# Up projections of two feed-forwards: seven block products of 256 tokens for each gate/up pair

## The chip, the cores and the metric

The kernel runs on 1 core of a Trainium2 chip. The metric is the device time of one execution in microseconds: 1858.99 us, median of 3 runs (1856.67 to 1860.89). Engines are named as the profile names them: PE (TensorE, matmuls; PEld its weight loads), DVE (VectorE), ACT (ScalarE), POOL (GpSimd), SP (SyncE, which issues the loads).

## The reference

512 tokens of 1024 channels in float32 go through three residual blocks, each a mixer and a feed-forward. The feed-forward of blocks two and three, around which this case turns, is

```
def swiglu_ffn(h, w13, w2):
    g, u = jnp.split(h @ w13, 2, axis=-1)
    return (jax.nn.silu(g) * u) @ w2
x = x + swiglu_ffn(rms_norm_2(x, norm_g), w13, w2)     # w13: 1024 x 5632, w2: 2816 x 1024
```

The feed-forward of block one has a causal convolution of three taps between the up projection and silu; the mixers (four kinds of heads, a gated convolution, latent attention) are not touched.

## The kernel before

Activations lie transposed, channels on partitions: `xT` is 8 tiles of 128 channels x 512 tokens. A float32 product is made of three fp32r passes: operand = hi + lo, and `passes` (L370 to L374) adds hi*hi, hi(weight)*lo(x) and lo(weight)*hi(x) in PSUM. A weight *unit* is 1024 x 128 of a matrix: one tile of 128 output channels. For each unit SP loads `raw` (4 slots, freed by `lo_split`), ACT copies `raw` to `whi` (`split_hi`, L359), DVE makes `wlo = raw - whi` (`split_lo`, L367), both with 2 slots, and PE runs 8 x 3 matmuls of 128x128 weights and 512 columns into one of two accumulator banks (`product`, L376 on). `unit_used` tells that PE is done with a unit, `acc_free` that its bank was read out.

In `ffn2_up` and `ffn3_up` units alternate: gate tile, up tile, 22 pairs, a loop of two pairs (`pe_up`, `act_up`, `dve_up`). DVE scales each result out of PSUM by the tokens' 1/rms (`zS = ps * rs`, L622), ACT applies silu to the gate (L605), DVE multiplies (`xg`, L638), ACT copies the product to `h_hi` (L608) and POOL makes `h_lo = xg - h_hi` (L647, `pool_products`). The gain of the norm is in `xhi`, `xlo` already; 1/rms comes later through `rs`: POOL sums squares (L563), PE adds over partitions (L400, `pe_sum`, behind the first unit), ACT takes Ln and Exp (`act_rstd`, L408, L410), with a table load before (L406) and one for silu after (L588).

The order on each engine is the order in which its function issues; engines meet by semaphores alone. A wait that precedes an instruction holds all behind it on that engine.

## Time and profile before

| | |
|---|---|
| median of 3 runs | 1858.99 us |
| the profiled execution | 1858.89 us, span 1857.1 us, mean clock of PE 0.997 |
| ffn2_up, 924.6 to 1164.0 us | 239.4 us; PE busy 239.4, DVE 98.3, ACT 76.7, POOL 28.7 |
| ffn3_up, 1484.0 to 1724.0 us | 240.0 us; PE busy 239.1, DVE 99.7, ACT 76.5, POOL 29.9 |

A matmul's time in the profile is its latency; matmuls overlap, so the pace of PE is the distance of their starts. Times on POOL are rougher than on the others.

### The profile page before, as it was taken

The page shows a single profiled execution, that of the slowest core. Times are in us where ns is not written, and L with a number is a line of the kernel's source. Part 1 is how long each engine was busy: PE and PEld are TensorE (multiplying, and loading weights), DVE is VectorE, ACT ScalarE, POOL GpSimd, SP SyncE. Part 2 cuts the span into 40 slices and gives each one's busy share as a digit, 9 for nine tenths or more (in the row PEclk, how much of TensorE's full clock was granted, in tenths as well). Part 3 has the DMA queues.
Part 4 walks back from the last instruction along what each step waited for, and adds up shares of the span by engine and source line. Part 5 has one row for each costly group of instructions (what it writes and reads, how often), then busy time and mean ns, then how long its engine had stood idle before and what let it go on. Part 6 is the DMA issues. An engine that isn't in the chain of part 4 may idle for free.

```text
span 1857.1 us, 27371 instructions
## 1 busy us (share of the span) xinstructions
PE 1823.2 (98%) x10063; PEld 1475.5 (79%) x10063; DVE 916.8 (49%) x1277; ACT 716.6 (39%) x1059; POOL 210.2 (11%) x181
## 2 busy tenths in 40 slices
...
DMA packets 309228, 161.03 MB, mean 87 GB/s; under 512 B 12688, under 2 KB 306832, under 8 KB 309024
## 3 DMA queue, kind: packets, MB, share of 16 engines
...
q8 instruction: 54, 0.88, 0.2%
...
## 4 chain that ended last, share of the span: by engine, by line
PE 94%; DVE 2%; ACT 2%; issue 1%; POOL 0%; DMA 0%; ACTq 0%; POOLq 0%; DVEq 0%
PE ps L372 28%; PE ps L374 28%; PE ps L373 28%; PE ps L1780 1%; PE ps L1191 1%; PE ps L2093 1%; PE ps L2094 1%; PE ps L1771 1%; PE ps L1102 1%; PE ps L1508 1%; PE ps L924 1%; PE ps L1452 1%; DVE xlo L446 0%; PE ps L1496 0%; PE ps L1877 0%
## 5 line engine op out<-in xcount | busy, mean ns | idle before, releaser
L372 PE MATMUL ps<-xhi,whi 128*128 128x512 f32 x1656 | 653.5, 395 | 2.0 <-DVE xlo L831 1.1
L374 PE MATMUL ps<-xhi,wlo 128*128 128x512 f32 x1656 | 644.8, 389 | 0.0
L373 PE MATMUL ps<-xlo,whi 128*128 128x512 f32 x1656 | 644.6, 389 | 0.0
L359 ACT ACTIVATE whi<-raw 128x1024 fp32r<-128x1024 f32 (+2 forms) x297 | 309.0, 1040 | 709.4 <-PE ps L374 708.8
L367 DVE TENSOR_TENSOR wlo<-raw,whi 128x1024 fp32r<-128x1024 f32 (+2 forms) x297 | 365.6, 1231 | 272.5 <-ACT whi L359 272.5
L372 PEld LDWEIGHTS ps<-xhi,whi 128*128 128x128 f32 x1656 | 310.9, 188 | 70.2 <-issue 4.3
L373 PEld LDWEIGHTS ps<-xlo,whi 128*128 128x128 f32 x1656 | 311.0, 188 | 65.9 <-issue 3.2
L374 PEld LDWEIGHTS ps<-xhi,wlo 128*128 128x128 f32 x1656 | 310.9, 188 | 65.4
L622 DVE TENSOR_TENSOR zS<-ps,rs 128x512 f32<-128x512 f32 x132 | 91.3, 692 | 296.9 <-PE ps L374 284.3
L374 PE MATMUL ps<-h_hi,wlo 128*128 128x512 f32 x528 | 205.4, 389 | 0.0
L372 PE MATMUL ps<-h_hi,whi 128*128 128x512 f32 x528 | 205.4, 389 | 0.0
L373 PE MATMUL ps<-h_lo,whi 128*128 128x512 f32 x528 | 205.4, 389 | 0.0
L647 POOL TENSOR_TENSOR h_lo<-xg,h_hi 128x512 f32 x66 | 85.4, 1293 | 639.3 <-ACT h_hi L608 639.3
L563 POOL TENSOR_TENSOR ssq<-ssq,sq 128x512 f32<-128x512 f32 x48 | 78.7, 1639 | 556.2 <-ACT sq L511 556.2
L373 PEld LDWEIGHTS ps<-h_lo,whi 128*128 128x128 f32 x528 | 99.1, 188 | 20.7
L372 PEld LDWEIGHTS ps<-h_hi,whi 128*128 128x128 f32 x528 | 99.1, 188 | 20.6
L374 PEld LDWEIGHTS ps<-h_hi,wlo 128*128 128x128 f32 x528 | 99.1, 188 | 20.4
L608 ACT ACTIVATE h_hi<-xg 128x512 f32 x66 | 41.7, 632 | 144.7 <-DVE xg L638 144.7
L544 DVE TENSOR_TENSOR xT<-ps,xT 128x512 f32<-128x512 f32 (+1 forms) x48 | 33.2, 691 | 120.3 <-PE ps L374 120.3
L446 DVE SCALAR_TENSOR_TENSOR xlo<-xT,pcol,xhi 128x512 fp32r<-128x512 f32 (+1 forms) x48 | 47.1, 1008 | 12.6 <-ACT xhi L440 12.6
L440 ACT ACTIVATE xhi<-xT,pcol 128x512 fp32r<-128x512 f32 (+1 forms) x48 | 32.8, 717 | 4.4 <-DVE xT L544 1.0
L511 ACT ACTIVATE sq<-xT 128x512 f32<-128x512 f32 (+1 forms) x48 | 29.9, 624 | 11.1 <-DVE xT L544 10.3
...
## 6 DMA issues: line engine op xcount, KB each, us to landing
...
```

Of the source, the lines that this page charges most:

```text
L359: a.activation(whi[:, u % PARTS, 0:n], raw[:, u % RAW, 0:n], ACT.Copy).then_inc(hi_split, 1)
L367: e.tensor_tensor(wlo[:, u % PARTS, 0:n], raw[:, u % RAW, 0:n], f32(whi[:, u % PARTS, 0:n]), ALU.subtract).then_inc(lo_split, 1)
L372: t_.matmul(out, wh, xh, start=first, stop=False)
L373: t_.matmul(out, wh, xl, start=False, stop=False)
L374: return t_.matmul(out, wl, xh, start=False, stop=last)
L440: a.activation(tile_of(xT if name == "final_norm_g_2" else xhi, k), tile_of(xT, k), ACT.Copy, scale=gain_of(name, k)).then_inc(x_hi, 1)
L446: v.scalar_tensor_tensor(tile_of(xlo, k), tile_of(xT, k), gain_of(name, k), f32(tile_of(xhi, k)), ALU.mult, ALU.subtract).then_inc(x_lo, 1)
L544: v.tensor_tensor(x, acc(m), x, ALU.add).then_inc(acc_free, 1)
L563: g.tensor_tensor(ssq[:, :], ssq[:, :], sq[:, m, :], ALU.add).then_inc(summed, 1)
L608: a.activation(tile_of(h_hi, m), xg[:, pair, :], ACT.Copy).then_inc(prod_hi, 1)
L622: v.tensor_tensor(z, acc(j), rs[:, :], ALU.mult).then_inc(acc_free, 1)
L647: g.tensor_tensor(tile_of(h_lo, m + 2 * i), xg[:, m, :], f32(tile_of(h_hi, m + 2 * i)), ALU.subtract).then_inc(prod_lo, 1)
```

## The change

In `ffn2_up` and `ffn3_up` pairs 0, 1, 20 and 21 stay as they were. The 18 between are computed by Strassen's method (the form with 15 sums): the operands are a 2x2 of blocks, weights (gate, up) x (channels 0 to 511, 512 to 1023), tokens (0 to 255, 256 to 511) x the same halves of the channels. Seven products of four row blocks and 256 tokens take the place of eight. Names: `HU` is half a unit (512 elements a partition), `HT` 256 tokens.

- Sums of the tokens, `t1` to `t4`, once a stage: made by POOL, ACT (scaled by the gain) and DVE at its start, then split into `t_hi` (ACT) and `t_lo` (POOL); their room is the end of `h`.
- Sums of the weights, four a pair, all on POOL: two in `xg` (L755, L757), one in place of the up tile's first half in `raw` (L758), one in place of the gate tile's second half (L765); ACT and DVE split them (`w_hi`, `w_lo`).
- Sums of the products: ACT copies two of them out of PSUM (`m1`, `m5`, in `sq`), DVE adds (L879, L882, L890, L896, L900), POOL adds two (L774, L778). Then come the scaling by `rs` (L892 gate, L903 up), now from SBUF, and the product with silu (L871), now straight into `h`.
- The lo parts of `h`, before made by POOL behind each pair, are made after the last of the 18 pairs, 22 in a row (L791), and the hi parts by ACT among the last four units. `h_hi` and `h_lo` have changed places in memory.
- PE waits before the first product of a pair for `acc_free` (the gate's L892 of the pair before) and for the gate's lo part (L865); before the second, fifth and sixth for the other lo parts, before the sixth also for L903.
- Stage start: ACT does the sums' copies ahead of `act_rstd`.

```diff
+HU, HT = UNIT // 2, T // 2
+SEVEN_END = FT // 2 - 1
+SEVEN_PAIRS = 2 * (SEVEN_END - 1)
+SEVEN0 = {"ffn2_up": 0, "ffn3_up": 1}
+X_SUMS = ("t1", "t2", "t3", "t4")
...
+        def seven(stage, it, q, each):
+            return each * (SEVEN_PAIRS * SEVEN0[stage] + 2 * it + q - 2)
+        def w_part(buf, more, u, name):
+            g0, u0 = buf[:, u % PARTS, :], buf[:, (u + 1) % PARTS, :]
+            return {"g0": g0[:, 0:HU], "g1": g0[:, HU:UNIT], "s3": u0[:, 0:HU], "u1": u0[:, HU:UNIT],
+                    "s1": more[:, 0, :], "s2": more[:, 1, :], "s4": more[:, 2, :]}[name]
...
+        def pe_seven(pe, stage, it, q):
+            u, n0 = FIRST[stage] + 2 * q, TILE0[stage]
+            def multiply(n, w, x):
+                (xh, xl), wh, wl = x_part(x), w_part(whi, w_hi, u, w), w_part(wlo, w_lo, u, w)
+                for k in range(4):
+                    cols = slice(k * P, (k + 1) * P)
+                    last = passes(seven_bank(stage, n), wh[:, cols], wl[:, cols], xh[:, k, :], xl[:, k, :],
+                                  k == 0, k == 3)
+                return last
+            pe.wait_ge(acc_free, n0 + 2 * q + 4 * it + 1)
+            pe.wait_ge(sums_lo, seven(stage, it, q, 2) + 1)
+            multiply(0, "g0", "x11").then_inc(quarter_done, 1)
+            pe.wait_ge(sums_lo, seven(stage, it, q, 2) + 2)
+            multiply(1, "s2", "t2").then_inc(quarter_done, 1)
+            multiply(2, "s1", "t1").then_inc(quarter_done, 1)
+            multiply(3, "g1", "x21").then_inc(unit_used, 1)
+            pe.wait_ge(lo_split, u + 4 * it + 1)
+            multiply(4, "s4", "x22").then_inc(quarter_done, 1)
+            pe.wait_ge(lo_split, u + 4 * it + 2)
+            pe.wait_ge(acc_free, n0 + 2 * q + 4 * it + 2)
+            multiply(5, "s3", "t3").then_inc(quarter_done, 1)
+            multiply(6, "u1", "t4").then_inc(unit_used, 1)
...
+            for n in X_SUMS:
+                pe.wait_ge(*after(f"{stage} {n} lo"))
+            with pe.Fori(1, SEVEN_END) as it:
...
+        def act_x_sums_made(act, stage, gain):
+            act.wait_ge(unit_used, FIRST[stage])
+            for k in range(4):
+                act.wait_ge(acc_free, TILE0[stage] + 2)
+                last = a.activation(tf["t3"][:, k, :], xT[:, k, HT:T], ACT.Copy, scale=par(gain, k))
+            last.then_inc(*step("act", f"{stage} x12"))
+            act.wait_ge(*after(f"{stage} d1"))
+            for k in range(4):
+                last = a.activation(tf["t1"][:, k, :], tf["t1"][:, k, :], ACT.Copy, scale=par(gain, k))
+            last.then_inc(*step("act", f"{stage} t1"))
+        def act_x_sums_hi(act, stage, names):
+            for n in names:
+                act.wait_ge(*after(f"{stage} {n}"))
+                a.activation(t_hi[:, X_SUMS.index(n), :, :], tf[n], ACT.Copy).then_inc(*step("act", f"{stage} {n} hi"))
+        def dve_x_sums(dve, stage, gain, name):
+            c0, less, ready = {"t3": (HT, "t3", "x12"), "t2": (HT, "t1", "t1"), "t4": (0, "t2", "t2")}[name]
+            dve.wait_ge(*after(f"{stage} {ready}"))
+            for k in range(4):
+                last = v.scalar_tensor_tensor(tf[name][:, k, :], xT[:, 4 + k, c0:c0 + HT], par(gain, 4 + k),
+                                              tf[less][:, k, :], ALU.mult, ALU.subtract)
+            last.then_inc(*step("dve", f"{stage} {name}"))
+        def pool_x_sums(pool, stage):
+            pool.wait_ge(unit_used, FIRST[stage])
+            pool.wait_ge(acc_free, TILE0[stage] + 2)
+            g.tensor_tensor(tf["t1"], xT[:, 0:4, HT:T], xT[:, 0:4, 0:HT],
+                            ALU.subtract).then_inc(*step("pool", f"{stage} d1"))
+            for n in ("t1", "t3", "t2", "t4"):
+                pool.wait_ge(*after(f"{stage} {n} hi"))
+                at = X_SUMS.index(n)
+                g.tensor_tensor(t_lo[:, at, :, :], tf[n], f32(t_hi[:, at, :, :]),
+                                ALU.subtract).then_inc(*step("pool", f"{stage} {n} lo"))
+        def pool_w_sums(pool, stage, it, q):
+            u = FIRST[stage] + 2 * q
+            gate, up = raw[:, u % RAW, :], raw[:, (u + 1) % RAW, :]
+            for n in range(2):
+                pool.wait_ge(unit_loaded[(u + n) % RAW], in_loop(LOADED[u + n], it, 64 // RAW))
+            pool.wait_ge(lo_split, u + 4 * it - 1)
+            g.tensor_tensor(xg[:, 0, :], up[:, 0:HU], up[:, HU:UNIT], ALU.add).then_inc(sums_made, 1)
+            pool.wait_ge(sums_made, seven(stage, it, q, 4) + 1)
+            g.tensor_tensor(xg[:, 1, :], xg[:, 0, :], gate[:, 0:HU], ALU.subtract).then_inc(sums_made, 1)
+            g.tensor_tensor(up[:, 0:HU], gate[:, 0:HU], up[:, 0:HU], ALU.subtract).then_inc(sums_made, 1)
+        def pool_last_w_sum(pool, stage, it, q):
+            u = FIRST[stage] + 2 * q
+            gate = raw[:, u % RAW, HU:UNIT]
+            pool.wait_ge(sums_lo, seven(stage, it, q, 2) + 1)
+            pool.wait_ge(sums_made, seven(stage, it, q, 4) + 2)
+            g.tensor_tensor(gate, gate, xg[:, 1, :], ALU.subtract).then_inc(sums_made, 1)
+        def pool_seven(pool, stage, it, q, zS, more):
+            at = 2 * it + q
+            if more:
+                pool_w_sums(pool, stage, it + q, 1 - q)
+            pool.wait_ge(quarter_kept, seven(stage, it, q, 2) + 2)
+            pool.wait_ge(quarter_added, seven(stage, it, q, 5) + 1)
+            pool.wait_ge(gated, GATED0[stage] + at)
+            g.tensor_tensor(zS[:, 0, HT:T], kept["u2"], kept["m5"], ALU.add).then_inc(pool_added, 1)
+            if more:
+                pool_last_w_sum(pool, stage, it + q, 1 - q)
+            pool.wait_ge(quarter_added, seven(stage, it, q, 5) + 4)
+            g.tensor_tensor(zS[:, 1, HT:T], kept["u3"], kept["m5"], ALU.add).then_inc(pool_added, 1)
...
+        def act_w_sums(act, stage, it, q):
+            u = FIRST[stage] + 2 * q
+            act.wait_ge(sums_made, seven(stage, it, q, 4) + 2)
+            a.activation(w_hi[:, 0:2, :], xg[:, :, :], ACT.Copy).then_inc(sums_hi, 1)
+            act.wait_ge(sums_made, seven(stage, it, q, 4) + 4)
+            if not (isinstance(it, int) and it == 1 and q == 0):
+                act.wait_ge(quarter_done, seven(stage, it, q, 5) - 1)
+            a.activation(w_hi[:, 2, :], raw[:, u % RAW, HU:UNIT], ACT.Copy).then_inc(sums_hi, 1)
+        def act_seven(act, stage, it, q, zS, yg, more):
+            u, n0 = FIRST[stage] + 2 * q, TILE0[stage]
+            act.wait_ge(sums_made, seven(stage, it, q, 4) + 3)
+            split_hi(act, u + 1, it, 4)
+            act.wait_ge(quarter_done, seven(stage, it, q, 5) + 1)
+            act.wait_ge(acc_free, n0 + 2 * q + 4 * it + 1)
+            a.activation(kept["m1"], seven_bank(stage, 0), ACT.Copy).then_inc(quarter_kept, 1)
+            act.wait_ge(quarter_done, seven(stage, it, q, 5) + 3)
+            act.wait_ge(acc_free, n0 + 2 * q + 4 * it + 2)
+            a.activation(kept["m5"], seven_bank(stage, 2), ACT.Copy).then_inc(quarter_kept, 1)
+            split_hi(act, u + 2, it, 4)
+            if more:
+                act_w_sums(act, stage, it + q, 1 - q)
+            act_silu_gate(act, stage, q, it, 2, zS, yg)
...
+        def dve_w_sums(dve, stage, it, q, first):
+            u = FIRST[stage] + 2 * q
+            n = seven(stage, it, q, 2)
+            if first:
+                dve.wait_ge(sums_hi, n + 1)
+                v.tensor_tensor(w_lo[:, 0:2, :], xg[:, :, :], f32(w_hi[:, 0:2, :]), ALU.subtract).then_inc(sums_lo, 1)
+            else:
+                dve.wait_ge(sums_hi, n + 2)
+                v.tensor_tensor(w_lo[:, 2, :], raw[:, u % RAW, HU:UNIT], f32(w_hi[:, 2, :]),
+                                ALU.subtract).then_inc(lo_split, 1)
+        def dve_gate_lo(dve, stage, it, q):
+            u = FIRST[stage] + 2 * q
+            dve.wait_ge(hi_split, u + 4 * it + 1)
+            v.tensor_tensor(wlo[:, u % PARTS, :], raw[:, u % RAW, :], f32(whi[:, u % PARTS, :]),
+                            ALU.subtract).then_inc(sums_lo, 1)
+        def dve_product(dve, stage, m, h, zS, yg, at):
+            dve.wait_ge(acc_free, TILE0[stage] + 2 * at + 4)
+            dve.wait_ge(gated, GATED0[stage] + at + 1)
+            v.tensor_tensor(tile_of(h, at), yg[:, m % 2, :], zS[:, 1, :], ALU.mult).then_inc(prod_done, 1)
+        def dve_seven(dve, stage, it, q, h, zS, yg, more):
+            u, at = FIRST[stage] + 2 * q, 2 * it + q
+            d0, a0, k0 = (seven(stage, it, q, n) for n in (5, 5, 2))
+            split_lo(dve, u + 1, it, 4)
+            dve.wait_ge(quarter_done, d0 + 2)
+            dve.wait_ge(quarter_kept, k0 + 1)
+            v.tensor_tensor(kept["u2"], seven_bank(stage, 1), kept["m1"], ALU.add).then_inc(quarter_added, 1)
+            dve.wait_ge(unit_used, u + 4 * it + 1)
+            dve.wait_ge(gated, GATED0[stage] + at)
+            v.tensor_tensor(zS[:, 0, 0:HT], seven_bank(stage, 3), kept["m1"], ALU.add).then_inc(quarter_added, 1)
+            if more:
+                dve_gate_lo(dve, stage, it + q, 1 - q)
+                dve_w_sums(dve, stage, it + q, 1 - q, True)
+            else:
+                split_lo(dve, u + 2, it, 4)
+            dve.wait_ge(quarter_done, d0 + 4)
+            dve.wait_ge(pool_added, k0 + 1)
+            v.tensor_tensor(zS[:, 0, HT:T], seven_bank(stage, 4), zS[:, 0, HT:T], ALU.add).then_inc(quarter_added, 1)
+            dve.wait_ge(quarter_added, a0 + 3)
+            v.tensor_tensor(zS[:, 0, :], zS[:, 0, :], rs[:, :], ALU.mult).then_inc(acc_free, 1)
+            if more:
+                dve_w_sums(dve, stage, it + q, 1 - q, False)
+            dve.wait_ge(quarter_done, d0 + 5)
+            v.tensor_tensor(kept["u3"], seven_bank(stage, 5), kept["u2"], ALU.add).then_inc(quarter_added, 1)
+            dve.wait_ge(unit_used, u + 4 * it + 2)
+            dve.wait_ge(prod_done, PAIR0[stage] + at + 2)
+            dve.wait_ge(quarter_added, a0 + 4)
+            v.tensor_tensor(zS[:, 1, 0:HT], seven_bank(stage, 6), kept["u3"], ALU.add).then_inc(quarter_added, 1)
+            dve.wait_ge(quarter_added, a0 + 5)
+            dve.wait_ge(pool_added, k0 + 2)
+            v.tensor_tensor(zS[:, 1, :], zS[:, 1, :], rs[:, :], ALU.mult).then_inc(acc_free, 1)
+            dve_product(dve, stage, q, h, zS, yg, at)
...
+        kept = {"m1": sq[:, 0, 0:HT], "m5": sq[:, 0, HT:T], "u2": sq[:, 1, 0:HT], "u3": sq[:, 1, HT:T]}
...
-            pool_products(pool, "ffn2_up", FT, h_hi, h_lo)
+            pool_up_seven(pool, "ffn2_up", h, h_lo, h_hi, zS3)
...
+            act_x_sums_made(act, "ffn2_up", "conv_ffn_norm_g_2")
+            act_x_sums_hi(act, "ffn2_up", ("t1", "t3"))
             act_rstd(act, "ffn2 norm", D, rs[:, :])
-            act_up(act, "ffn2_up", False, h_hi, zS, yg, yu)
+            act_up_seven(act, "ffn2_up", h, h_lo, zS3, yg3)
```

DVE in `ffn2_up`, kernel before: the first of the two pairs in the loop. `zS` is the scaled result, `xg` the product.

```order
L622 TENSOR_TENSOR zS<-ps,rs 128x512 [waits prod_done]
L366 REGISTER_ALU
L367 TENSOR_TENSOR wlo<-raw,whi 128x1024 [waits hi_split]
L624 REGISTER_ALU
L617 REGISTER_ALU [waits acc_free]
L622 TENSOR_TENSOR zS<-ps,rs 128x512 [waits prod_done,unit_used]
L366 REGISTER_ALU
L367 TENSOR_TENSOR wlo<-raw,whi 128x1024 [waits hi_split]
L624 REGISTER_ALU
L636 REGISTER_ALU [waits acc_free]
L637 REGISTER_ALU [waits gated]
L638 TENSOR_TENSOR xg<-yg,zS 128x512 [waits prod_lo]
```

The same engine and place now, from the first sum of products to the last lo part of the next pair's weights. `sq` holds m1, m5, u2, u3.

```order
L879 TENSOR_TENSOR sq<-ps,sq 128x256 [waits quarter_kept,quarter_done]
L882 TENSOR_TENSOR zS<-ps,sq 128x256 [waits gated,unit_used]
L864 ISA
L865 TENSOR_TENSOR wlo<-raw,whi 128x1024 [waits hi_split]
L855 ISA
L856 TENSOR_TENSOR w_lo<-xg,w_hi 128x1024 [waits sums_hi]
L888 REGISTER_ALU
L890 TENSOR_TENSOR zS<-ps,zS 128x256 [waits pool_added,quarter_done]
L891 REGISTER_ALU
L892 TENSOR_TENSOR zS<-zS,rs 128x512 [waits quarter_added]
L858 REGISTER_ALU
L859 TENSOR_TENSOR w_lo<-raw,w_hi 128x512 [waits sums_hi]
```

Between two scalings stood a split; now two additions out of PSUM stand before the next gate's lo part and the sums' lo parts, and the scaling L892 follows all of these. Behind these rows come L896, L900, L903 and L871 of the up tile.

POOL in `ffn2_up`, kernel before: the loop's first operation, the lo part of the product.

```order
L644 UNCONDITIONAL_BRANCH
L644 ISA
L647 ISA [waits prod_hi]
L647 TENSOR_TENSOR h_lo<-xg,h_hi 128x512
L646 REGISTER_ALU
```

POOL in the loop now, one pair: `raw` and `xg` are weights' sums, `sq` and `zS` products' sums.

```order
L754 ISA [waits unit_loaded2]
L755 TENSOR_TENSOR xg<-raw 128x512 [waits lo_split]
L756 ISA
L757 TENSOR_TENSOR xg<-xg,raw 128x512 [waits sums_made]
L758 TENSOR_TENSOR raw<-raw 128x512
L771 REGISTER_ALU
L772 ISA [waits quarter_kept]
L773 REGISTER_ALU [waits quarter_added]
L774 TENSOR_TENSOR zS<-sq 128x256 [waits gated]
L763 ISA
L764 REGISTER_ALU [waits sums_lo]
L765 TENSOR_TENSOR raw<-raw,xg 128x512 [waits sums_made]
```

One operation of 512 elements a pair became four of 512 and two of 256 (the second is L778, behind these rows), and the lo part of the product left the loop.

## Rows read from the trace of the kernel before

**Rows 1.** The page, part 1: engine, busy us (share of the span), instructions.
```profile
PE 1823.2 (98%) x10063; PEld 1475.5 (79%) x10063; DVE 916.8 (49%) x1277; ACT 716.6 (39%) x1059; POOL 210.2 (11%) x181
```

**Rows 2.** The page, part 4: the chain that ended last, shares by engine.
```profile
PE 94%; DVE 2%; ACT 2%; issue 1%; POOL 0%; DMA 0%; ACTq 0%; POOLq 0%; DVEq 0%
```

**Rows 3.** Busy time by stretch: ffn2_up (columns: stretch, length, engines, clock, DMA share, GB/s).
```profile
924.60:1164.00 239.40, 239.40 (x1056) 197.92 (x1055) 98.33 (x110) 76.67 (x93) 28.71 (x22) 1.00 0.32 95
```

**Rows 4.** Timeline of PE in ffn2_up: start us, us, engine, line, shapes, count.
```profile
1130.05 0.39 PE L372 MATMUL ps<-xhi,whi 128*128 128x512 f32 x1
...
1140.93 0.39 PE L372 MATMUL ps<-xhi,whi 128*128 128x512 f32 x1
```

**Rows 5.** Timeline of PE in the attention of the third block, plain fp32 matmuls.
```profile
1397.44 0.60 PE L2093 MATMUL ps<-kn,qn 128*128 128x256 f32 x2
...
1397.87 0.59 PE L2094 MATMUL ps<-kpz,qp 128*128 128x256 f32 x2
...
1410.21 0.39 PE L2094 MATMUL ps<-kpz,qp 128*128 128x128 f32 x2
...
1410.44 0.38 PE L1771 MATMUL ps<-cst,mla_P 128*128 128x128 f32 x2
```

**Rows 6.** Timeline of ACT and DVE in one unit of ffn2_up.
```profile
1137.73 1.06 ACT L359 ACTIVATE whi<-raw 128x1024 fp32r<-128x1024 f32 x1 [1.75 <-PE ps L374]
...
1137.82 0.69 DVE L622 TENSOR_TENSOR zS<-ps,rs 128x512 f32<-128x512 f32 x1 [2.61 <-PE ps L374]
...
1138.83 1.23 DVE L367 TENSOR_TENSOR wlo<-raw,whi 128x1024 fp32r<-128x1024 f32 x1 [0.31 <-ACT whi L359]
```

**Rows 7.** Timeline of DVE and POOL where they meet, ffn1_up and conv_out.
```profile
472.28 0.69 DVE L622 TENSOR_TENSOR zS<-ps,rs 128x512 f32<-128x512 f32 x1 [0.77 <-PE ps L374]
...
472.46 1.30 POOL L647 TENSOR_TENSOR h_lo<-xg,h_hi 128x512 f32 x1 [9.57 <-ACT h_hi L608]
...
473.29 1.55 DVE L367 TENSOR_TENSOR wlo<-raw,whi 128x1024 fp32r<-128x1024 f32 x1 [0.32 <-ACT whi L359]
...
909.45 1.23 DVE L367 TENSOR_TENSOR wlo<-raw,whi 128x1024 fp32r<-128x1024 f32 x1 [0.29 <-ACT whi L359]
...
910.15 1.66 POOL L563 TENSOR_TENSOR ssq<-ssq,sq 128x512 f32<-128x512 f32 x1 [3.78 <-ACT sq L511]
...
911.03 1.34 DVE L446 SCALAR_TENSOR_TENSOR xlo<-xT,pcol,xhi  x1 [0.36 <-ACT xhi L440]
```

**Rows 8.** Groups by line and form: 256 elements out of PSUM, DVE and ACT.
```profile
L1603 DVE TENSOR_TENSOR mx<-ps,cst 128x256 f32<-128x256 f32 x24 | 8.7, 414 | 0.0
...
L1206 ACT ACTIVATE mx<-ps 128x256 f32<-128x256 f32 x20 | 7.7, 384 | 22.0 <-PE ps L1102 20.8
```

**Rows 9.** Timeline of the start of ffn2_up.
```profile
925.70 0.63 ACT L511 ACTIVATE sq<-xT 128x512 f32 x1
...
926.49 1.65 POOL L563 TENSOR_TENSOR ssq<-ssq,sq 128x512 f32<-128x512 f32 x1 [3.79 <-ACT sq L511]
...
927.22 1.28 ACT L406 ACT_TABLE_LOAD   x1
...
930.98 0.69 ACT L408 ACTIVATE rs<-ps,cst 128x512 f32<-128x512 f32 x1 [2.48 <-PE ps L400]
...
931.70 0.63 ACT L410 ACTIVATE rs<-rs 128x512 f32<-128x512 f32 x1
...
934.74 1.23 DVE L367 TENSOR_TENSOR wlo<-raw,whi 128x1024 fp32r<-128x1024 f32 x1 [1.03 <-ACT whi L359]
...
936.24 0.40 PE L372 MATMUL ps<-xhi,whi 128*128 128x512 f32 x1
```

**Rows 10.** Busy time by stretch around a fall of PE's clock.
```profile
329.00:332.00 3.00, 1.48 (x9) 1.13 (x10) 1.40 (x4) 1.46 (x4) 0.00 (x0) 0.95 0.00 0
...
332.00:335.00 3.00, 3.00 (x6) 1.25 (x5) 0.12 (x1) 0.30 (x1) 0.00 (x0) 0.50 0.02 5
```

133 lines of the change are left out of this document (118 added, 15 removed).

## The prediction

> **What bounds the kernel now.** I read the busy shares first: TensorE (PE) is busy 98% of the span, 1823.2 us, VectorE (DVE) 49%, ScalarE (ACT) 39%, GpSimd (POOL) 11% [rows 1]. The chain of waits that ended last says the same by another road: 94% of it is PE [rows 2]. Then the table by stretch: the up projection of feed-forward two, 924.6 to 1164.0 us, runs at clock 1.00 with PE busy all of its 239.4 us, DVE 98, ACT 77 and POOL 29 [rows 3]; that of feed-forward three is the same loop. So PE sets the pace in both, and the other engines hide behind it. A busy PE row is latency, not throughput, so the pace is read from starts: 48 matmuls of 512 columns, one gate/up pair, lie between 1130.05 and 1140.93 us. That is 10.88 us a pair or 0.227 us a matmul [rows 4]; 22 pairs make the 239.4 us. DVE has two splits of 1.23 us, two scalings of 0.69 and one product per pair, and is idle for more than half of the time [rows 6].
>
> **The change, PE's part.** A pair becomes 7 products of 4 blocks of rows in 3 passes: 84 matmuls of 256 columns instead of 48 of 512, the columns falling by one eighth. No fp32r matmul of 256 columns stands in the trace. Bounds: not below 0.110 us, the pace of full 128x128 weights with 128 columns each (two matmuls from 1410.21 to 1410.44 [rows 5]); not above 0.215, what plain fp32 takes for 256 columns (two from 1397.44 to 1397.87 [rows 5]). Half of 0.227 is 0.113; if the part above 512 columns at 2.4 GHz (0.213 us) is paid per matmul, it is 0.120. I take 0.117, between those two: 84 x 0.117 = 9.8 us a pair. If PE stayed the bound, 1.1 us a pair would be won.
>
> **What it puts on DVE and POOL.** Per pair DVE now has L376, L865, L856 (1024 elements, 1.23 us each by the split's row), L892, L859, L903, L871 (512 elements, 0.69 each) and L879, L882, L890, L896, L900 (256 elements from PSUM, 0.415 each by the L1603 row) [rows 6, 8]. Independent ones start 0.08 us early; sum 7.9 us. POOL has L755, L757, L758, L765 (512 elements, 1.29 each; L647 took 1.30 [rows 7]) and L774, L778 (256 elements; not shown for two inputs, estimate 0.14 start + half of 1.15 = 0.71): 6.6 us. ACT has three copies of 1024 at 1.06 [rows 6] and four small ones of 0.4 to 0.6: 5.2 us. Each engine alone is below 9.8. The question is whether they run beside each other.
>
> They do not. At 473.29 a DVE split began while POOL's L647 ran from 472.46 to 473.76; the split ended at 474.84, 1.08 us after POOL's end, and took 1.55 us where 1.23 is normal. The other way round, POOL's L563 began at 910.15 under a split that ended at 910.68, and ended 1.13 us after it (1.66 us in all); the next DVE operation, L446, ended 0.56 us after that. But L622, which reads PSUM and one SBUF tile, kept its 0.69 us beside L647 [rows 7]. So a DVE operation with both inputs in SBUF and a POOL operation follow each other, whoever is first: after the other's end a 1024 split costs 1.08 us, a 512 operation 0.55, a POOL 512 operation 1.14 (1.13 in this row) and (estimate) a POOL 256 one 0.57. Before the change POOL had 22 operations in the whole stage [rows 3]; now every POOL operation and seven DVE operations of a pair are of this kind: 3 x 1.08 + 4 x 0.55 + 4 x 1.14 + 2 x 0.57 = 11.1 us. Even packed without a hole that is more than the 10.88 us of the pair before.
>
> The Trainium skill (SBUF — State Buffer, section "Who interferes with whom") states this as a rule: a DVE instruction with two SBUF inputs and a GpSimd instruction that reads SBUF take one shared pair of ports as an exclusive lock, and a DVE instruction with one SBUF input is left alone. By that rule, the trace agrees (1.08 us after POOL's end, and 0.69 us unchanged for L622), the time is the one summed here; without it the change would give rival B's.
>
> **One round, step by step.** It is not packed, because of what waits for what. From the end of L865 (lo of the next gate):
> L856 1.15; L765 on POOL, which waited for L865 and then for L856, 1.14; L892, which wants the port too, 0.55; L859 waits for ACT's copy L801 of what L765 made (0.63 + two hops of 0.1) and takes 0.69, so 1.03 beyond L892; L896 0.34 (0.415 less the early start); POOL's L778 waits for it, 0.17 hop (L563 starts 0.16 after L511's end [rows 9]) + 0.71 = 0.88, while L900 is hidden; then POOL's next sums and DVE's three operations take turns: L755 1.29, L903 0.55, L757 1.14, L871 0.55, L758 1.14, L376 1.08; L879 0.33; POOL's L774 waits for it, 0.88 (L882 is hidden); the next L865, behind L774, 1.08. Sum: 1.15 + 1.14 + 0.55 + 1.03 + 0.34 + 0.88 + 1.29 + 0.55 + 1.14 + 0.55 + 1.14 + 1.08 + 0.33 + 0.88 + 1.08 = 13.1 us. No matmul is in it. PE (9.8 us) waits 3.3 us a round: some 2.3 before the first product of a pair, which needs L892 (L681 waits for acc_free, and the 84 matmuls are queued behind it), and 1.0 before the sixth, which needs L376.
>
> The last pair of a stage has no next pair to prepare; I count 17 rounds a stage: 34 x (13.1 - 10.88) = +75.5 us. The two last pairs are taken at no change.
>
> **Start of each stage.** ACT's queue now holds, ahead of the rstd, four scaled copies (L718), four more (L722) that wait for POOL's difference, and two copies of 1024 (L728). Before: ACT turns to the rstd's table at 927.22, the rstd is done at 932.33, the split of the third unit ends with L367 at 935.97, and PE takes that unit at 936.24, 0.3 us later [rows 9]. Now: four copies at about 0.4 (as L1206, [rows 8]) to 928.8; POOL's d1, four times 256 elements, 0.14 + 4 x 0.575 = 2.4, from L563's end at 928.14, and 0.5 for hops and for DVE operations in its way: to 931.1; four copies 932.7; two of 1.06: 934.9; table 1.28, Ln 0.69, Exp 0.63, table 1.28, split 1.06, DVE's split 1.23: 941.1. PE stands 5.0 us. Later steps of the start have units two and three (10.9 us) to hide in. Two stages: +10 us; between 6 and 16, as the turns with POOL go. POOL's 22 h_lo at the end (1.29 each, 28 us) hide behind four units (21.8 us) and the down projection's first 10 us, since block k = 15 is needed only then: nothing. A unit's load has a pair's time before anyone asks for it, and DMA is busy 0.32 of that stage [rows 3]: nothing.
>
> **Sum.** 1858.9 (this execution's own time: its span of 1857.1 and 1.8 around it; 0.1 below the median of the runs) + 75.5 + 10 = 1944 us.
>
> **Rivals.**
> B, the two engines do run beside each other: then the round is PE's products one to four (48 x 0.117 = 5.6), ACT's split of the next gate (0.2 + 1.06), L865, L856 (2.3), L890 0.42, L892 0.15 + 0.69, and PE's restart 0.25: 10.65 us, since product one waits for L892. 36 x (-0.23) + 10: 1861. Against it: every meeting in rows 7.
> C, the turns pack better than I laid them: POOL's sums slip in while DVE does its PSUM operations. Between 11.2 and 12.3 a round: 34 x 0.3 or 1.4 + 10: 1880 to 1917. For it: 7.9 us of DVE include 2 us of PSUM work that could cover POOL. Against: L778 and L774 wait for just those.
> D, the faster side: PE stays the bound, everything else hides, from the point where L892 ends within three products (4.2 us) of the fourth's end. 36 x (9.8 - 10.88) + 10 = -29: 1830 (at 0.113, 1820). Against: in B's chain alone it ends 4.8 us after it.
> E, 256 columns run at plain fp32's pace, 0.215: 84 x 0.215 = 18.1 a pair, 36 x 7.2 + 10 = +269: 2128. Nothing in the trace speaks for it, but nothing excludes it.
> F, the gaps of 2.3 us take PE's clock down: between 329 and 332 us PE was busy 1.48 of 3 us, and its clock stood at 0.50 in the three us behind [rows 10]. PE has some 2 us of slack in my round before L882 would wait, so a drop of 3 us costs little; if each round had one and paid 1 us, +34: 1978.
>
> **Chances.** My round (12.3 to 13.5 us) 0.70; C 0.13; F 0.07; B 0.04; D 0.03; E 0.03. The likeliest gives 1944. Its own range is 1917 to 1960; with C's upper part and F it becomes 1905 to 1980, and what is left out is about 0.17. A measurement of this kernel can tell about 0.2%, 3.7 us. Faster: D and a piece of B, 0.04. Same: the rest of B, 0.03. Slower: 0.93.
>
> **What would show it.** In the changed profile: PE's busy share of both stages falls to some 75 to 80%; PE waits for zS from L892 by about 2 us and for wlo from L376 by about 1, 34 times or so; L376 lasts up to 2.3 us, L903 and L871 about 1.6 on average, POOL's L765 2.1; L879 to L900 stay at 0.42; the first units of each stage show one PE gap of 5 us. I am wrong if L903 stays at 0.69 beside a running POOL operation, if the starts of 256-column matmuls are over 0.13 us apart, or if PE shows no gaps.

## The result, and the profile after

The changed kernel takes 1945.0 us (median of four runs, 1944.2 to 1946.2), the kernel before 1858.8 in the same session: ratio 1.0463, 95% interval [1.0449, 1.0478]. It is 86 us slower; 1944 was predicted. The profiled execution has a span of 1944.3 us, 87.2 more than before. Line numbers of the changed kernel are some 9 above those of before in the old code (L372 to L374 are L381 to L383, L367 is L376, L359 is L368); the scaling L622 is L912.

Busy shares (page, part 1) and chain (part 4) of the changed kernel, against [rows 1, 2]:

```profile
PE 1828.4 (94%) x11359; PEld 1533.6 (79%) x11359; DVE 1216.5 (63%) x1553; ACT 807.5 (42%) x1227; POOL 548.1 (28%) x407
```

```profile
PE 71%; DVE 11%; POOL 8%; issue 7%; ACT 2%; DVEq 0%; DMA 0%; POOLq 0%; ACTq 0%
```

PE's share of the chain fell from 94 to 71%. What came in is DVE, POOL and PE's issue: PE now waits, and no other engine fills the chain in its place. That is a first hint, not more, that the engines take turns.

Busy time by stretch in ffn2_up of the changed kernel (columns as in [rows 3]):

```profile
924.60:950.00 25.40, 19.72 (x79) 15.51 (x78) 22.25 (x21) 16.34 (x23) 16.61 (x7) 0.87 0.24 68
950.00:1203.00 253.00, 219.91 (x1620) 210.21 (x1619) 223.97 (x228) 105.23 (x153) 164.52 (x119) 0.97 0.28 83
```

PE was busy all of the stage before [rows 3]; DVE now is for 224 of 253 us and POOL for 165. (An operation's row also holds the time in which it waits for the other engine, as the rows below show.) From the first matmul of the second unit, the one behind the sum over partitions (L409), to the first of the down projection, the stage takes 275.0 us, 234.35 before; ffn3_up takes 278.2, 234.3 before. That is 84.6 of the 87.2 us.

PE's pace, timeline of the changed kernel (start, us):

```profile
1000.92 0.28 PE L381 MATMUL ps<-t_hi,whi 128*128 128x256 f32 x1
...
1003.33 0.28 PE L383 MATMUL ps<-t_hi,wlo 128*128 128x256 f32 x1
```

The second row's start is 20 matmuls behind the first's: 0.1205 us each, against 0.227 with 512 columns [rows 4]. A pair is 84 x 0.120 = 10.08 us: the saved multiplications do give PE 0.8 us a pair. What the other engines now do costs more than that.

Groups by line and form in 960 to 1180 us of the changed kernel (busy, mean ns | idle before):

```profile
L376 DVE TENSOR_TENSOR wlo<-raw,whi 128x1024 fp32r<-128x1024 f32 x17 | 38.2, 2247 | 0.0
...
L903 DVE TENSOR_TENSOR zS<-zS,rs 128x512 f32<-128x512 f32 x17 | 28.3, 1666 | 6.1 <-POOL zS L778 6.1
...
L900 DVE TENSOR_TENSOR zS<-ps,sq 128x256 f32<-128x256 f32 x17 | 7.2, 425 | 1.8
```

L376 took 1.23 us before [rows 6] and takes 2.25. L903, the scaling of 512 elements, takes 1.67; from PSUM it took 0.69 [rows 6], and from SBUF it takes 0.69 too where POOL leaves it alone (e1). L900, with an input in PSUM, keeps 0.42. Only operations with both inputs in SBUF became longer.

One round on DVE and POOL, timeline of the changed kernel:

```profile
1053.06 1.32 DVE L865 TENSOR_TENSOR wlo<-raw,whi 128x1024 fp32r<-128x1024 f32 x1 [0.33 <-ACT whi L368]
1054.31 1.21 DVE L856 TENSOR_TENSOR w_lo<-xg,w_hi 128x1024 fp32r<-128x1024 f32 x1
1054.54 2.12 POOL L765 TENSOR_TENSOR raw<-raw,xg 128x512 f32<-128x512 f32 x1 [1.24 <-DVE wlo L865]
...
1055.89 1.32 DVE L892 TENSOR_TENSOR zS<-zS,rs 128x512 f32<-128x512 f32 x1
...
1057.44 0.69 DVE L859 TENSOR_TENSOR w_lo<-raw,w_hi 128x512 fp32r<-128x512 f32 x1 [0.23 <-ACT w_hi L801]
...
1058.05 0.42 DVE L896 TENSOR_TENSOR sq<-ps,sq 128x256 f32<-128x256 f32 x1
1058.55 0.74 POOL L778 TENSOR_TENSOR zS<-sq 128x256 f32<-128x256 f32 x1 [1.88 <-DVE sq L896]
...
1059.25 1.30 POOL L755 TENSOR_TENSOR xg<-raw 128x512 f32<-128x512 f32 x1
1059.39 1.70 DVE L903 TENSOR_TENSOR zS<-zS,rs 128x512 f32<-128x512 f32 x1 [0.40 <-POOL zS L778]
...
1060.63 1.62 POOL L757 TENSOR_TENSOR xg<-xg,raw 128x512 f32<-128x512 f32 x1
1061.32 1.47 DVE L871 TENSOR_TENSOR h<-yg,zS 128x512 f32 x1 [0.23 <-DVE zS L903]
...
1062.21 1.74 POOL L758 TENSOR_TENSOR raw<-raw 128x512 f32<-128x512 f32 x1
1062.71 2.31 DVE L376 TENSOR_TENSOR wlo<-raw,whi 128x1024 fp32r<-128x1024 f32 x1
...
1065.52 0.74 POOL L774 TENSOR_TENSOR zS<-sq 128x256 f32<-128x256 f32 x1 [1.57 <-DVE sq L879]
1065.62 1.73 DVE L865 TENSOR_TENSOR wlo<-raw,whi 128x1024 fp32r<-128x1024 f32 x1
```

Read it by ends (start plus duration, here without the leading 10). L856 ends at 55.52, L765 at 56.66, L892 at 57.21, L859 58.13, L896 58.47, L778 59.29, L755 60.55, L903 61.09, L757 62.25, L871 62.79, L758 63.95, L376 65.02, L774 66.26, L865 67.35. Where the engine changes from one operation to the next, the second ends a fixed time behind the first, however long ago it started: 1.14 to 1.16 us for POOL's 512 elements, 0.54 or 0.55 for DVE's, 1.07 to 1.09 for a split. The other steps wait for a result: L859 for ACT's copy of what L765 made (0.92), L778 for L896 (0.82), L774 for DVE's L879 (1.24 from L376's end, L879 included). The chain stands still only at these hops: 0.23 us ahead of L859, 0.1 to 0.2 ahead of L778 and L774. No matmul is in it.

PE's waits, whole changed kernel (us in total, times, longest):

```profile
PE ps L381 <- DVE zS L892: 59.4, 34, 2.0
PE ps L381 <- DVE wlo L376: 20.6, 25, 7.0
```

Start of ffn2_up, timeline of the changed kernel, against [rows 9]:

```profile
931.20 1.71 ACT L722 ACTIVATE h<-h,pcol 128x256 f32<-128x256 f32 x4 [2.17 <-POOL h L741]
...
932.95 7.49 DVE L734 SCALAR_TENSOR_TENSOR h<-xT,pcol,h 128x256 f32<-128x256 f32 x8 [0.31 <-ACT h L722]
...
934.97 1.28 ACT L415 ACT_TABLE_LOAD   x1
...
940.96 1.21 DVE L376 TENSOR_TENSOR wlo<-raw,whi 128x1024 fp32r<-128x1024 f32 x1
...
942.31 0.77 PE L381 MATMUL ps<-xhi,whi 128*128 128x512 f32 x1 [5.68 <-DVE wlo L376]
942.88 0.63 PE L382 MATMUL ps<-xlo,whi 128*128 128x512 f32 x1
```

The rstd's table is loaded at 934.97 instead of 927.22, and PE stands 5.68 us. Behind the gap its matmuls are 0.43 us apart instead of 0.227.

PE in short stretches of the changed kernel (length, PE busy, granted clock, DMA): the start, then the middle of the loop.

```profile
939.00:942.00 3.00, 0.00 (x0) 0.51 0.00 0
942.00:945.00 3.00, 2.69 (x6) 0.50 0.49 139
945.00:948.00 3.00, 3.00 (x13) 0.85 0.23 65
```

```profile
1043.00:1046.00 3.00, 1.57 (x9) 0.81 0.00 0
1046.00:1049.00 3.00, 3.00 (x18) 0.62 0.59 174
1049.00:1052.00 3.00, 3.00 (x27) 1.00 0.00 0
```

The clock falls to its lower level, 1.2 of 2.4 GHz, within the start's gap, and PE's matmuls stay slow for 3.6 us behind it, until 945.87 (4.7 us in ffn3_up, behind a gap of 6.95). In the loop it falls for 3 to 4 us at a time, 5 times in each stage's 18 pairs. Before, it stood at 1.00 throughout the stage [rows 3].

### The profile page after: what moved, and what is told of

It is laid out like the page before. It is cut to its first block, busy times and chain, and to the rows that moved or that the text cites. A ratio compares the mean times of both kernels' runs of the same rounds, so it can differ in the third digit from the quotient of the medians.

```text
span 1944.3 us, 31272 instructions
## 1 busy us (share of the span) xinstructions
PE 1828.4 (94%) x11359; PEld 1533.6 (79%) x11359; DVE 1216.5 (63%) x1553; ACT 807.5 (42%) x1227; POOL 548.1 (28%) x407
## 3 DMA queue, kind: packets, MB, share of 16 engines
q0 software_dynamic: 640, 2.17, 0.3%
## 4 chain that ended last, share of the span: by engine, by line
PE 71%; DVE 11%; POOL 8%; issue 7%; ACT 2%; DVEq 0%; DMA 0%; POOLq 0%; ACTq 0%
PE ps L381 21%; PE ps L383 20%; PE ps L382 20%; POOL h_hi L791 4%; POOL raw L765 2%; DVE wlo L865 2%; DVE zS L903 2%; PE ps L2075 1%; DVE wlo L376 1%; DVE zS L892 1%; DVE w_lo L856 1%; PE ps L1486 1%; ACT whi L368 1%; PE ps L2392 1%; PE ps L2393 1%
## 5 line engine op out<-in xcount | busy, mean ns | idle before, releaser
L381 PE MATMUL ps<-xhi,whi 128*128 128x512 f32 (+1 forms) x1368 | 519.8, 380 | 73.7 <-DVE zS L892 59.4
L368 ACT ACTIVATE whi<-raw 128x1024 fp32r<-128x1024 f32 (+2 forms) x297 | 308.1, 1037 | 529.2 <-PE ps L383 528.6
L376 DVE TENSOR_TENSOR wlo<-raw,whi 128x1024 fp32r<-128x1024 f32 (+2 forms) x261 | 366.8, 1406 | 243.7 <-ACT whi L368 243.7
L383 PE MATMUL ps<-xhi,wlo 128*128 128x512 f32 (+1 forms) x1368 | 507.7, 371 | 0.0
L382 PE MATMUL ps<-xlo,whi 128*128 128x512 f32 (+1 forms) x1368 | 507.5, 371 | 0.0
L381 PEld LDWEIGHTS ps<-xhi,whi 128*128 128x128 f32 x1368 | 261.6, 191 | 128.1 <-issue 83.8
L383 PEld LDWEIGHTS ps<-xhi,wlo 128*128 128x128 f32 x1368 | 262.7, 192 | 43.0
L572 POOL TENSOR_TENSOR ssq<-ssq,sq 128x512 f32<-128x512 f32 x48 | 78.7, 1640 | 538.9 <-ACT sq L520 538.9
L381 PE MATMUL ps<-h_lo,whi 128*128 128x512 f32 x352 | 137.4, 390 | 1.2 <-POOL h_hi L791 1.2
L383 PE MATMUL ps<-h_lo,wlo 128*128 128x512 f32 x352 | 136.9, 389 | 0.0
L381 PE MATMUL ps<-t_hi,whi 128*128 128x256 f32 x288 | 83.7, 291 | 7.9 <-DVE wlo L376 7.9
L765 POOL TENSOR_TENSOR raw<-raw,xg 128x512 f32<-128x512 f32 x36 | 76.6, 2127 | 39.5 <-DVE wlo L865 39.5
L381 PE MATMUL ps<-t_hi,w_hi 128*128 128x256 f32 x288 | 85.3, 296 | 0.0
L382 PE MATMUL ps<-t_lo,w_hi 128*128 128x256 f32 x288 | 84.9, 295 | 0.0
L383 PE MATMUL ps<-t_hi,w_lo 128*128 128x256 f32 x288 | 84.5, 293 | 0.0
L382 PE MATMUL ps<-t_lo,whi 128*128 128x256 f32 x288 | 81.4, 283 | 0.0
L383 PE MATMUL ps<-t_hi,wlo 128*128 128x256 f32 x288 | 81.3, 282 | 0.0
```

The costliest lines, as they stand in the source:

```text
L368: a.activation(whi[:, u % PARTS, 0:n], raw[:, u % RAW, 0:n], ACT.Copy).then_inc(hi_split, 1)
L376: e.tensor_tensor(wlo[:, u % PARTS, 0:n], raw[:, u % RAW, 0:n], f32(whi[:, u % PARTS, 0:n]), ALU.subtract).then_inc(lo_split, 1)
L381: t_.matmul(out, wh, xh, start=first, stop=False)
L382: t_.matmul(out, wh, xl, start=False, stop=False)
L383: return t_.matmul(out, wl, xh, start=False, stop=last)
L572: g.tensor_tensor(ssq[:, :], ssq[:, :], sq[:, m, :], ALU.add).then_inc(summed, 1)
```

## Experiments

Theory T: DVE and POOL do their SBUF work in turns, the chain of turns is the round, and PE waits for it. Each experiment is an edit of the changed kernel; of each edit the lines that carry it are shown. "Before" is 1858.4 us beside the first four, 1856.0 beside e5 and e6, 1857.5 beside e7 and e8, 1857.2 beside e9.

**e1_short_pool.** All waits and signals stay, but POOL's six operations of a pair work on 16 columns, so the kernel leaves out nearly all of their sums; two VectorE operations of unchanged size (L892 and L905 here) read `sq` where those sums would have been. One of the six:

```diff
-            g.tensor_tensor(xg[:, 0, :], up[:, 0:HU], up[:, HU:UNIT], ALU.add).then_inc(sums_made, 1)
+            g.tensor_tensor(xg[:, 0, 0:16], up[:, 0:16], up[:, HU:HU + 16], ALU.add).then_inc(sums_made, 1)
```

> The changed kernel, but POOL's six operations per pair (L755, L757, L758, L765, L774, L778) work on 16 columns instead of 512 and 256; their results are mostly left out, all waits stay. Theory T (DVE and POOL take turns at one port, the round of 12.9 us is that chain): the round falls to the chain through L892, 48 x 0.120 + 5.1 = 10.85 us, 34 x -2.08 = -71: 1874 us, and PE still waits for L892, now below 1 us. Rival R (DVE's twelve operations of 7.9 us and their waits on ACT are too much by themselves): the round stays within 0.5 us of 12.9, 1928 to 1945. Rival P (256-column matmuls or the clock set the round): 1945.

Measured: 1871.3 us, ratio 1.0064 [1.0047, 1.0081]. The gate's lo (L867 here) and the scaling L903 (L905 here):

```profile
1050.45 1.22 DVE L867 TENSOR_TENSOR wlo<-raw,whi 128x1024 fp32r<-128x1024 f32 x1 [0.58 <-ACT whi L368]
...
1061.16 1.23 DVE L867 TENSOR_TENSOR wlo<-raw,whi 128x1024 fp32r<-128x1024 f32 x1 [0.67 <-ACT whi L368]
```

```profile
L905 DVE TENSOR_TENSOR zS<-sq,rs 128x512 f32<-128x512 f32 x18 | 12.5, 692 | 1.3
```

A round is 10.71 us, 2.22 less than 12.93: 34 x 2.22 = 75.5 us, and the time fell by 74. DVE's operations have their old lengths. PE still waits 0.4 us at the start of each pair (for L894, which is L892 of the changed kernel, 34 times, 13.1 us).

**e2_pool_writes_only.** POOL is busy about as long, but reads one column in place of 256 or 512; the sums are left out. One of the six operations:

```diff
+        def hold(at, n=HOLD):
+            g.tensor_tensor(idle_tile[:, at * HOLD:at * HOLD + 1], C("ones")[:, 0:1], C("ones")[:, 0:1], ALU.subtract)
+            g.memset(idle_tile[:, at * HOLD + 1:at * HOLD + n], 0.0)
...
-            g.tensor_tensor(xg[:, 0, :], up[:, 0:HU], up[:, HU:UNIT], ALU.add).then_inc(sums_made, 1)
+            hold(0); g.memset(xg[:, 0, :], 0.5).then_inc(sums_made, 1)
```

> The changed kernel, but each of POOL's six operations per pair is replaced by one of 1 column and two memsets that together last as long (1.29 us for the 512 ones, about 0.7 us for the 256 ones); the sums are left out, all waits stay, POOL reads nothing of size from SBUF. Theory T, with the port as cause: two memsets do not stand in DVE's way, L376 and L903 return to 1.23 and 0.69 us, the round falls to 10.85 us and the time to 1874, as in e1. Rival S (POOL's time counts because it is in series in the chain, not because of a port): L376 and L903 return to normal only by chance, the round stays at 12 to 13 us, 1914 to 1945 us.

Measured: 1869.3 us, ratio 1.0057 [1.0041, 1.0074]. POOL's idle writes, and DVE's second scaling (L903, here L908):

```profile
L653 POOL MEMSET idle_tile<- 128x619 f32 x68 | 41.7, 613 | 0.0
```

```profile
L908 DVE TENSOR_TENSOR zS<-zS,rs 128x512 f32<-128x512 f32 x18 | 12.5, 693 | 3.7 <-POOL zS L783 3.7
```

POOL is busy 121 of the 190 us between 960 and 1150, within the loop, as in the changed kernel (121), and DVE does not feel it; the round is 10.71 us as in e1. So it is neither that POOL works nor its place in the chain, but the operations that read their inputs from SBUF. The Trainium skill (SBUF — State Buffer, "Who interferes with whom") states the lock for GpSimd instructions that read SBUF, and not for those that only write it. This run agrees: 0.693 us beside writes, 1.67 beside reads.

**e3_two_passes.** The third pass of the seven products is left out (so low parts of the weights are missing in the output), a third of PE's work in a pair:

```diff
-                    last = passes(seven_bank(stage, n), wh[:, cols], wl[:, cols], xh[:, k, :], xl[:, k, :],
-                                  k == 0, k == 3)
+                    t_.matmul(seven_bank(stage, n), wh[:, cols], xh[:, k, :], start=k == 0, stop=False)
+                    last = t_.matmul(seven_bank(stage, n), wh[:, cols], xl[:, k, :], start=False, stop=k == 3)
```

> The changed kernel with the third pass (hi(x) x lo(weight)) left out of the seven products: 56 instead of 84 matmuls a pair, 6.7 instead of 10.1 us of PE. Theory T: no matmul is in the round, so it stays at 12.9 us; only the last pair of each stage, which has no next pair to prepare, gets up to 3.4 us shorter: 1938 to 1945 us. Rival P (PE, its 256-column pace or its clock has a share in the round): 36 x 3.4 = 121 us less at most, 1824; anything below 1930 speaks for a share of PE. PE idles half of the round here; should its clock stay low for long, 56 matmuls at half clock are 12 us and still fit.

Measured: 1942.2 us, ratio 1.0455 [1.0436, 1.0474]. 28 matmuls a pair less are 36 x 3.4 = 121 us of PE's work; the time is 2.8 us less than the changed kernel's, and a round is 12.91. The granted clock was 0.86 over the loop (950 to 1203 us) and cost nothing either. PE only waits longer:

```profile
PE ps L677 <- DVE zS L892: 98.5, 34, 4.8
```

**e4_rstd_first.** ScalarE makes the rstd (`between` below), loads silu's table and makes the third unit's split right behind its first copies; VectorE makes t2 behind the first unit and t4 behind the second:

```diff
             last.then_inc(*step("act", f"{stage} x12"))
+            between()
+            a.preload_act_table_set("silu_and_others")
+            split_hi(act, FIRST[stage] + 2)
```

> The changed kernel with the stage start in another order: ACT does rstd, the table load and the third unit's split before the copies that wait for POOL's difference, and DVE scales and splits units one and two between the tokens' sums. Nothing is left out. Theory T, start term: the PE gaps of 5.8 and 7.1 us ahead of the third unit go, 1945 - 12 = 1933 us, if the tokens' sums are still ready when the fifth unit ends. Rival: they are not (POOL's four lo parts are 10 us of its time), the gap only moves ahead of the first pair of seven: 1940 to 1948 us.

Measured: 1948.1 us, ratio 1.0479 [1.0461, 1.0496]: nothing gained, where 1933 was expected. PE's waits between 924 and 960 us, the start of ffn2_up:

```profile
PE ps L381 <- DVE wlo L868: 3.2, 1, 3.2
PE ps L381 <- DVE w_lo L859: 1.9, 1, 1.9
PE ps L381 <- DVE wlo L376: 1.8, 1, 1.8
```

The gap of 5.7 is 1.8 now, and two new ones stand at the first seven products, whose operands are late by as much: 6.9 in all. The rival held. My reading that the order of ScalarE's queue alone made the gap was wrong.

**e5_sums_on_vector.** All six SBUF operations of a pair go to VectorE, which is the busiest of the helpers already:

```diff
+            if more:
+                pool_w_sums(dve, stage, it + q, 1 - q, v)
...
+            v.tensor_tensor(zS[:, 0, HT:T], kept["u2"], kept["m5"], ALU.add).then_inc(pool_added, 1)
...
+                pool_last_w_sum(dve, stage, it + q, 1 - q, v)
...
+            v.tensor_tensor(zS[:, 1, HT:T], kept["u3"], kept["m5"], ALU.add).then_inc(pool_added, 1)
```

> All six SBUF operations that GpSimd does for a pair (L755, L757, L758, L765, L774, L778) stand in VectorE's order instead; GpSimd keeps only the first pair's sums of a stage and the h_lo at its end. VectorE, at 63% of the span already, gets four more of 512 elements (0.61 each beyond the early start) and two of 256. Theory T (the turns at the port make the 12.93 us round): a round has no turn left, VectorE needs 7.9 + 4 x 0.61 + 2 x 0.34 = 11.0 us and the hops to and from ScalarE some 0.5 more: 11.5 us. 34 x (11.5 - 12.93) = -49: 1896 us (1885 to 1910), VectorE busy 95% of the loop, L376 at 1.23 and L903 at 0.69. A rival (VectorE's own work and its order make the round, GpSimd's share is a relief): the moved 3.1 us are added to a VectorE that is already busy 223 of 253 us, the round is 14 us or more, the time 1980 or more.

Measured: 1893.9 us, ratio 1.0199 [1.0182, 1.0216]. The gate's lo (L860 here) and PE's wait:

```profile
1052.44 1.22 DVE L860 TENSOR_TENSOR wlo<-raw,whi 128x1024 fp32r<-128x1024 f32 x1
...
1063.90 1.22 DVE L860 TENSOR_TENSOR wlo<-raw,whi 128x1024 fp32r<-128x1024 f32 x1
```

```profile
PE ps L381 <- DVE zS L892: 36.9, 34, 1.1
```

A round is 11.46 us (11.5 expected). One engine doing all of it is 1.47 us a round faster than two that share it, with the same arithmetic. It is still above 10.88: some 11 us of work a pair stand on one engine, which is busy 95% of the loop.

**e6_both_moves.** e5 with the start of e4.

> The sums of a pair on VectorE as in e5_sums_on_vector, and the start of each stage in the order of e4_rstd_first (ScalarE: rstd, silu table and split of the third unit ahead of its other copies). With the order of e4_rstd_first alone the 5.7 and 6.9 us of gap moved behind the third unit, where TensorE waited for the lo of the fourth unit and of the sums. Theory V (the gap is the sum of the copies, differences and sums that must be made before the first product, whatever their order): as e5_sums_on_vector within 4 us. Rival (the gap behind the third unit was made by the turns between L738 and GpSimd's L750 and the first sums): it shrinks where VectorE is alone with them, 5 to 12 us under e5_sums_on_vector. The first pair's sums of a stage are still GpSimd's, which speaks for V.

Measured: 1896.3 us, ratio 1.0215 [1.0198, 1.0232], 2.4 above e5: the waits of e4 stand there again (3.2, 2.3 and 1.8 us). Theory V held: in this loop another order only moves the gap.

**e7_every_second_pair.** The loop's body is a plain pair, then a pair of seven products; its sums, made by VectorE during the plain pair:

```diff
+            with dve.Fori(1, SEVEN_END) as it:
+                split_lo(dve, u0 + 1, it, 4)
+                pool_w_sums(dve, stage, it, 1, v)
+                unit(0, acc(0), False, it)
+                dve_gate_lo(dve, stage, it, 1)
+                dve_w_sums(dve, stage, it, 1, True)
+                pool_last_w_sum(dve, stage, it, 1, v)
+                unit(1, acc(1), False, it)
+                dve_w_sums(dve, stage, it, 1, False)
+                dve_seven(dve, stage, it, 1, h, zS, yg, False)
```

> Seven products only in every second pair (nine pairs a stage): of the pairs 2 to 19 each even one is a plain pair of 48 matmuls of 512 columns and each odd one has the 84 of 256. All sums are on VectorE as in e5_sums_on_vector, the start has the order of e4_rstd_first, and the sums of the inputs are needed 10.9 us later than there. Theory T: two pairs need VectorE for 11.0 + 3.9 = 14.9 us and TensorE for 84 x 0.120 + 10.88 = 20.96 us, so TensorE is the bound and never waits in the loop: 18 x (20.96 - 21.76) = -14.4 us. The start keeps the 1.8 us gap ahead of the third unit (1.5 a stage beyond the 0.3 of before, +3), and the wait for h_hi behind each stage stays (+2.4): 1856.0 - 14.4 + 3 + 2.4 = 1847 us (1843 to 1853), so faster than the kernel before. Rival (a pair of 84 small matmuls costs TensorE more than the sum of its pitches, because it waits at its restart however free the other engines are): 10.7 a pair as in e1_short_pool, 1858 us or more.

Measured: 1860.4 us, ratio 1.001 [1.0000, 1.0021]. That is outside T's range and where the rival put the time (1858 or more), but not by the rival's mechanism: PE has no wait in the loop, which did what T says (rows under e9). The start lost it, with gaps of 1.8 and 3.2 us in each stage and slow matmuls for 6.1 us (3.2 in ffn3_up) behind the second.

**e8_and_late_start.** The inputs' sums behind all that units three and four need (ScalarE: rstd, table, split, silu, split, then the copies).

> As e7_every_second_pair, and the sums of the inputs come behind everything that the third unit needs: ScalarE makes rstd, table, the third unit's split, the first silu and the fourth unit's split, and then the scaled copies; VectorE makes t3 and t2 behind the second unit, t4 behind the third. Theory T (the gap at the start is only queue order, once there is slack behind it): no gap ahead of the third unit beyond the 0.3 us of before, 3 us under e7_every_second_pair: 1844 us (1840 to 1850). Rival (the inputs' sums are as many microseconds of work and stall some unit wherever they stand, as in e4_rstd_first): as e7_every_second_pair within 2 us or slower, with the gap at the fourth or fifth unit.

Measured: 1858.6 us, ratio 1.0007 [0.9995, 1.0020], within 2 us of e7: T missed, and the rival held but for the place. The gap of 1.8 went, and one of 3.7 stands at the sixth unit, not at the fourth or fifth. Why, in the timeline of DVE and POOL; then PE and its clock behind it:

```profile
939.41 8.80 POOL L751 TENSOR_TENSOR t_lo<-h,t_hi 128x1024 fp32r<-128x1024 f32 x3 [11.01 <-ACT t_hi L733]
...
943.35 5.94 DVE L739 SCALAR_TENSOR_TENSOR h<-xT,pcol,h 128x256 f32<-128x256 f32 x4
```

```profile
953.96 0.79 PE L381 MATMUL ps<-xhi,whi 128*128 128x512 f32 x1 [3.74 <-DVE wlo L376]
```

```profile
956.00:959.00 3.00, 3.00 (x9) 0.50 0.49 144
```

Four small operations (t4) took 5.94 us beside GpSimd's differences of 1024 elements. The first two lasted 2.61 and 2.62 us, each ending 0.28 us behind one of the differences; the last two, with GpSimd done (948.21), lasted 0.47 each. In e4, where GpSimd stood still, the four took 1.66:

```profile
946.71 1.66 DVE L738 SCALAR_TENSOR_TENSOR h<-xT,pcol,h 128x256 f32<-128x256 f32 x4
```

**e9_no_turns_at_start.** The same, without that meeting (the lines against e8's kernel):

```diff
-                for n in ((), ("t3", "t2"), ("t4",), ())[j]:
+                for n in (("t3", "t2", "t4") if j == 1 else ()):
...
+            pool.wait_ge(*after(f"{stage} t4"))
             for n in ("t1", "t3", "t2", "t4"):
```

> As e8_and_late_start, with two changes at the start of a stage: VectorE makes t4 right behind t3 and t2, and GpSimd's four differences t_lo wait until t4 is made. In e8_and_late_start t4's four operations took 5.94 us in turns with GpSimd's (they took 1.66 in e4_rstd_first where GpSimd stood still); the lo of the sixth unit came 3.7 us late, and TensorE's clock stood at 0.50 for over 3 us behind the gap. Theory T (turns, and the clock behind a gap): no gap beyond 0.3 us in the first six units, clock 1.00 throughout the stage, and per stage 3.7 us of gap and 2 to 3 us of slow matmuls less: 1858.6 - 12 = 1847 us (1843 to 1851), under the kernel before. Rival (the gap moves once more, to the first of the seven products, because GpSimd now begins 3 us later): as e8_and_late_start or slower, 1858 us or more, with TensorE waiting for t_lo.

Measured: 1852.1 us (1849.9 to 1853.5), ratio 0.9973 [0.9962, 0.9984]: a little faster than the kernel before, and 1 us above the expected range. PE's timeline in its loop, where shapes change, and busy time by stretch:

```profile
1042.87 0.28 PE L381 MATMUL ps<-xhi,whi 128*128 128x256 f32 x1
...
1052.94 0.40 PE L381 MATMUL ps<-xhi,whi 128*128 128x512 f32 x1
...
1063.85 0.28 PE L381 MATMUL ps<-xhi,whi 128*128 128x256 f32 x1
```

```profile
924.60:1164.00 239.40, 237.34 (x1398) 210.57 (x1397) 178.07 (x241) 102.78 (x141) 41.37 (x22) 1.00 0.33 97
```

A pair of seven products takes 10.07 us, a plain one behind it 10.91: 9 x (20.98 - 21.76) = -7.0 us a stage. PE is full again, the clock 1.00. Three pieces of gap are left at the start, 0.6, 0.4 and 1.1 us a stage, while VectorE still takes turns with GpSimd's t_lo there (two of its splits, L376, last 3.05 and 3.41 us). Together they are 4.1 of the 5.1 us above 1847.

## Why the prediction was right, step by step

**PE's part.** 0.117 us a matmul was taken; 0.120 was measured, the upper of the two values it was chosen between. (The lower bound of 0.110 was misread: the two matmuls from 1410.21 to 1410.44 are 0.115 each.) It did not matter, PE being off the path (e3). Rival E (0.215) fell.

**Turns.** Every price stood (predicted in brackets): 1.07 for a split behind POOL (1.08), 0.54 for a DVE operation of 512 elements (0.55), 1.16 for POOL's (1.14), and L896 and L900 kept 0.42. They had been read from two chance meetings [rows 7]. e1 and e2 show that the cause is POOL's reading. Rivals B, C and D fall with them: in the loop PE's restarts lie 12.89 to 12.94 us apart. B's own number, 10.65 without turns, was good: e1 gives 10.71.

**The round.** Fifteen terms gave 13.1; the round above gives 12.97 and the mean is 12.93. Two terms were too long: L859 behind L892 0.92 (1.03), L778 0.82 (0.88). 34 x (12.93 - 10.88) = +69.7 us where 75.5 was predicted. The first round of a stage takes 11.8 us only, and the last pairs take 10.2 and 11.7, so that by PE's starts the 36 pairs cost +67.6 us.

**PE's waits.** Predicted 2 and 1 us, 34 times each: L892 34 times and 1.75 on average; L376 (20.6 - 12.6 at the starts) in 23 rounds only, 0.35 each. This sign came out too small. The rest of PE's slack is in slow matmuls and in restarts. PE's busy share of the loop is 87% (219.9 of 253 us), not 75 to 80.

**Start of a stage.** Mis-sized: 5.0 predicted, waits of 5.7 and 6.95 us measured, and with what follows them the starts cost 17.0 us together (84.6 less 67.6), not the likeliest 10 and just beyond the 6 to 16 allowed. ACT's part went as summed (its split ends at 939.99). Two things were left out: VectorE's eight operations for t2 and t4, which took 7.49 us in turns with POOL's t_lo and stood ahead of the third unit's lo (941.0 to 942.2, 941.1 predicted); and the clock behind the gap, where 8 and 11 matmuls some 0.43 us apart cost 4 us, both stages together. In ffn3_up POOL came to its first difference 1.5 us later (L741 starts at 1531.75, 0.7 us ahead of the second unit's first matmul, not 2.3; ACT waits 3.93 us for it, not 2.17), since its L572 took 2.81 us behind DVE's L455 and L376, not 1.66. The "0.5 for DVE operations in its way" was the term.

**POOL's h_lo at nothing.** Nearly: each down projection is 1.2 us longer, 0.6 of it in waits for L791.

**F.** The clock does fall, every second to fifth round, but PE's slack takes it: the rounds with a fall are not longer. Where there is no slack, it is not free. The last pair of ffn3_up, with a fall, takes 11.7 us, that of ffn2_up, without, 10.2. And at the starts e9's waits for operands of the two stages are 3.4 us shorter than e8's (4.1 and 7.5), its two stages are 6.6 us shorter in the profiles, and what else differs between PE's starts is e8's 22 slow matmuls.

The mechanism was right; that the number was met within 1 us is luck in part. The errors of the rounds and of the starts, -7.9 and +7.0 us, cancel, and 2.4 us behind the stages were not foreseen: 1944 was met more closely than its terms were.

**Left open.** The stretch ahead of ffn2_up, which no edit touches, takes from 2.5 us less (e8) to 3.0 us more (e1) than before. In e1 the two stages are only 9.3 us longer than before while its span is 14.6 longer. The clock has a part in this: between 20 and 900 us it stood at its lower level for 13.6 us in e1 and 13.8 in e2 (0.80 and 0.69 over the two 10 us from 120 us in e1), for 3.4 us in before, and never in e8. But among the eight profiles with 3.4 us the stretch still differs by almost 3 us. Why is not known. A mixture with two of three pairs in seven products was not run.
